# Query, key, value and gates of a hybrid attention block prepared between the input units and kept in DRAM

## What is computed

```python
h = rms_norm(x, g_mix)
q_down, kv_down, k_rope, conv_in, gate_logits = split(h @ w_in)    # 256, 128, 32, 1024, 2048 columns
q  = rms_norm(q_down, g_q_lora) @ w_uq                # 8 heads of 64 + 32 rotary
kv = rms_norm(kv_down, g_kv_lora) @ w_ukv             # 8 heads: 64 of k, 64 of v
k  = concat(k_nope, k_rope of all heads)
q, k = rope(rms_norm(q, g_qk_q)), rope(rms_norm(k, g_qk_k))
y_a = chunk_causal_attention(q, k, v) @ w_o_mla       # blocks of 128 queries, keys up to their own chunk of 64
u   = conv_value * sigmoid(conv_gate)
y_b = silu(layer_norm(depthwise_conv_31(u))) @ w_conv_out
gates = sigmoid(gate_logits + b_gates)                # two of width 1024
x = x + (gates[:D] * y_a + gates[D:] * y_b) @ w_out
x = x + experts(rms_norm(x, g_ffn))                   # 32 experts, two per token
```

## Time and profile before

| | |
|---|---|
| median of 3 runs | 1280.9 us (1279.85 to 1282.06) |
| profiled execution | 1280.47 us, span 1278.4 us |
| TensorE matmul busy | 1178.3 us, 92% of the span |
| VectorE, ScalarE, GpSimd busy | 751.0, 469.2, 198.9 us |
| chain that ended last | TensorE 71%, DMA 12%, ScalarE 4%, VectorE 4% |
| input units, attention, branches | 281, 269, 89 us |

### The profile page before, as it was taken

One profiled execution on the slowest core, in us unless ns is written; L12 is line 12 of the kernel. 1 busy time (PEld: TensorE's weight loads), 2 busy tenths in 40 slices (PEclk: granted clock), 3 DMA queues, 4 the chain that ended last, 5 costly groups with the idle time before them and its releaser, 6 DMA issues.

```text
span 1278.4 us, 14988 instructions
## 1 busy us (share of the span) xinstructions
PE 1178.3 (92%) x5452; PEld 896.4 (70%) x5452; DVE 751.0 (59%) x992; ACT 469.2 (37%) x635; POOL 198.9 (16%) x243
## 2 busy tenths in 40 slices
PE   5999999999968999999899899849999988989996
PEld 5988888887645667767788788746676665666664
DVE  3338999993424455444466434476776656656663
ACT  4432111113443444444232211124555544554552
POOL 4010000000142232220000000011222321222211
PEclk8999999999969999999799999958999999999999
DMA  6011111110100000001330233495999999999980
GB/s 224 1 50 50 49 49 49 49 49 17 42 0 1 1 1 1 1 1 34 131 83 17 90 113 129 169 320 179 324 339 320 304 322 316 334 333 314 308 267 8
DMA packets 101542, 172.28 MB, mean 135 GB/s; under 512 B 11727, under 2 KB 45690, under 8 KB 101498
## 3 DMA queue, kind: packets, MB, share of 16 engines
q1 hardware_dynamic: 91002, 154.86, 35.8%
q0 software_dynamic: 10432, 16.81, 5.4%
q10 hardware_dynamic: 64, 0.02, 0.0%
HBM read 165.35 MB, written 27.26 MB: 151 GB/s over the span
## 4 chain that ended last, share of the span: by engine, by line
PE 71%; DMA 12%; ACT 4%; DVE 4%; issue 4%; POOL 2%; SPq 2%; DVEq 0%; ACTq 0%; POOLq 0%
PE pb L1224 15%; PE pb L1226 15%; PE pb L1225 15%; DMA wgu_raw<-in_w_e_up 11%; PE pb L1506 7%; PE pb L1364 4%; PE pb L1341 4%; PE pb L1353 2%; PE pb L1273 2%; PE pb L1478 2%; PE pb L1283 1%; PE pb L1424 1%; ACT wgu_hi L772 1%; SPq L414 1%; SPq L418 1%
## 5 line engine op out<-in xcount | busy, mean ns | idle before, releaser
L1165 DVE TENSOR_TENSOR wgu_lo<-wgu_raw,wgu_hi 128x2048 fp32r<-128x2048 f32 x72 | 164.7, 2289 | 89.3 <-ACT wgu_hi L772 87.8
L1506 PE MATMUL pb<-wed,midT 128*128 128x512 f32 x288 | 136.5, 618 | 23.1 <-DVE midT L1200 23.0
L873 DVE SCALAR_TENSOR_TENSOR cv<-up,dwc,cv 128x1024 f32<-128x1024 f32 x120 | 154.1, 1284 | 3.7
L1224 PE MATMUL pb<-hT_hi,ws_hi 128*128 128x512 f32 x384 | 151.7, 395 | 0.0
L772 ACT ACTIVATE wgu_hi<-wgu_raw 128x2048 fp32r<-128x2048 f32 x72 | 137.1, 1909 | 38.0 <-DMA wgu_raw<-in_w_e_up 33.8
L1226 PE MATMUL pb<-hT_hi,ws_lo 128*128 128x512 f32 x384 | 149.5, 389 | 0.0
L1225 PE MATMUL pb<-hT_lo,ws_hi 128*128 128x512 f32 x384 | 149.5, 389 | 0.0
L1224 PE MATMUL pb<-wgu_hi,hgT_hi 128*128 128x512 f32 x288 | 130.0, 452 | 0.0
L1506 PEld LDWEIGHTS pb<-wed,midT 128*128 128x128 f32 x288 | 54.6, 196 | 87.2 <-issue 62.5
L1226 PE MATMUL pb<-wgu_hi,hgT_lo 128*128 128x512 f32 x288 | 113.2, 393 | 0.0
L1225 PE MATMUL pb<-wgu_lo,hgT_hi 128*128 128x512 f32 x288 | 112.5, 391 | 0.0
(11 more groups left out here) (281 smaller groups left out, 2019.9 us busy)
## 6 DMA issues: line engine op xcount, KB each, us to landing
wgu_raw<-in_w_e_gate SPq DMA_DIRECT2D x36, 1024.0 KB
wgu_raw<-in_w_e_up SPq DMA_DIRECT2D x36, 1024.0 KB
wed<-in_w_e_down SPq DMA_DIRECT2D x36, 1024.0 KB, 16.3
ws_raw<-in_w_in SPq DMA_DIRECT2D x24, 512.0 KB, 3.9
xs<-in_x SPq DMA_DIRECT2D x8, 512.0 KB, 8.4
wout<-in_w_out SPq DMA_DIRECT2D x1, 4096.0 KB, 12.9
xb<-in_x SPq DMA_DIRECT2D x8, 512.0 KB, 5.2
h_rows<-h SPq DMA_DIRECT2D x8, 512.0 KB, 2.7
```

Source lines behind the costliest of these rows:

```text
L873: i = v.scalar_tensor_tensor(out=cv[:, c, :], in0=src, scalar=w, in1=cv[:, c, :], op0=ALU.mult, op1=ALU.add)
L1165: v.tensor_tensor(wgu_lo[q % SLOTS][:, :, ks, :], wgu_raw[q % SLOTS][:, :, ks, :], wgu_hi[q % 2][:, :, ks, :].bitcast(F32), ALU.subtract). ...
L1224: t_.matmul(out, w(0), m(0), start=start, stop=False)
L1506: m = t_.matmul(pb[:, 4 + h, :], midT[:, f, :], wed[q][:, f, h * 512:(h + 1) * 512], start=(f == 0), stop=(f == 1))
```

## The change

- Preparation (now `prep`) of tile t starts in unit 1+2t and runs over 32 steps, in the order of `PREP` at the steps `PREP_STEP`. TensorE has two banks for it (6 and 7, in turn), VectorE's program has its pieces two steps later (`PREP_LAG`) among the taps, ScalarE's has them after the split for the unit after next. The squares are now made in PSUM, and VectorE sums them in halves.
- q, k and v go to staging tiles (`qst`, `kst`, `vst`), are stored to DRAM, and are loaded again for attention (q two tiles at a time). Gates go through two staging rows (`gst`) to DRAM and come back for the branches.
- The scores of heads 0 and 1 go into unit 23 at its steps 2 and 6, behind the convolution's layer norm; the exponentials of both follow the convolution's swish on ScalarE.
- Attention has no preparation left. `attn_T` transposes the output tile; ScalarE and VectorE split it straight from PSUM into `aT`. The convolution's result is split at heads 9 to 12. The first branch unit starts with its convolution half; the last output tile is transposed between its two halves.
- The rotary angles and tables are computed ahead of unit 0's evacuation and right after it, rather than at units 1 and 19.
- The unit loops are written out; the matmuls of the units are the same.

```diff
+        PREP = ("qdT", "q0", "q1", "kv0", "kv1", "qT0", "qT1", "kT0", "kT1")
+        PREP_STEP = (0, 3, 6, 9, 12, 22, 24, 28, 30)
+        PREP_UNIT, PREP_LAG = 1, 2
+        prep_at = {STEPS * PREP_UNIT + 2 * STEPS * t + g: (k, t) for t in range(NTILE) for k, g in zip(PREP, PREP_STEP)}
...
 # SyncE
+                store_gate(u - 4)
+                sp.wait_ge(u_hi, u - 1)
+                sp.wait_ge(u_lo, u - 1)
+                load_unit(u % 2, unit_col(u))
+                store_prep(u - 4)
...
+            sp.wait_ge(ln_y, NC)
+            sp.dma_start(vv[:, :, :], v_d.rearrange("t p c -> p t c")).then_inc(v_in, 16)
...
+            sp.wait_ge(pv_ok, NTILE * HEADS)
...
+            load_gates(0)
+            load_gates(1)
 # ScalarE
                 if u + 2 < IN_UNITS:
                     unit_hi(u + 2)
+                for s in range(STEPS):
+                    if STEPS * (u + 1) + s in prep_at:
+                        prep(*prep_at[STEPS * (u + 1) + s])
 # VectorE
                 if u + 2 < IN_UNITS:
                     unit_lo(u + 2)
+                if u == 0:
+                    rotary_tables()
...
+                fresh = max(0, target - taps_done)
+                for s in range(STEPS):
+                    for k in range(taps_done + fresh * s // STEPS, taps_done + fresh * (s + 1) // STEPS):
+                        tap(k)
+                    if STEPS * (u + 1) + s - PREP_LAG in prep_at:
+                        prep(*prep_at[STEPS * (u + 1) + s - PREP_LAG])
 # TensorE
+                    if kind == "q0":
+                        bb, cc = prep_slot("qdT", t)
+                        pe.wait_ge(prep_free[bb], cc)
...
+            def unit(u):
+                b = u % 2
                 for f in range(2):
                     for k in range(KD):
+                        if STEPS * u + f * KD + k in prep_at:
+                            prep(*prep_at[STEPS * u + f * KD + k])
+                        if u == IN_UNITS - 1 and f == 0 and k in (2, 6):
+                            pe.wait_ge(ln_sd, 1)
+                            pe.wait_ge(ln_y, 1)
+                            scores(k // 4)
                         i = three(pb[:, 2 * b + 2 + f, :], lambda s: ws[s][:, b, k, :], lambda s: hT[s][:, k, f * 512:(f + 1) * 512], k == 0, k == KD - 1)
...
                 probs_T(n)
-                for k, t in slots(j, h, 0):
-                    misc(k, t)
                 if n + 2 < NTILE * HEADS:
                     scores(n + 2)
-                for k, t in slots(j, h, 1):
-                    misc(k, t)
+                if j and h == 2:
+                    attn_T(j - 1)
                 pv(n)
...
+            branch(0, 1)
+            attn_T(NTILE - 1)
+            pe.wait_ge(at_lo, NTILE)
+            branch(0, 0).then_inc(u_mm, 1)
```

More of the change, by code:

```diff
@@ L60 @@
 TAPS_PER_UNIT = 7
+STEPS = 2 * KD
 LO_SPLIT = 5
@@ L324, in build, with prep_slot @@
         EARLY = ((NTILE - 1) * HEADS + 4, (NTILE - 1) * HEADS + 5)
[L326 to L337, removed]
+        CONV_SPLIT = (9, 10, 11, 12)
+        PREP = ("qdT", "q0", "q1", "kv0", "kv1", "qT0", "qT1", "kT0", "kT1")
+        PREP_STEP = (0, 3, 6, 9, 12, 22, 24, 28, 30)
+        PREP_UNIT, PREP_LAG = 1, 2
+        prep_at = {STEPS * PREP_UNIT + 2 * STEPS * t + g: (k, t) for t in range(NTILE) for k, g in zip(PREP, PREP_STEP)}
+        def prep_slot(kind, t):
+            n = len(PREP) * t + PREP.index(kind)
+            return n % 2, n // 2 + 1
+        SBANK = (0, 6)
         SMALL_VECS = ((V_GM, g_mix, 8), (V_BG, b_gates, 16), (V_BD, b_dw, 4), (V_GL, g_conv_ln, 4),
@@ L384, in _, with unit_col, prep_freed, store_prep @@
-            sp.wait_ge(u_hi, IN_UNITS)
-            sp.wait_ge(u_lo, IN_UNITS)
+            def unit_col(u):
+                if u < GLU_UNITS:
+                    return (VALUE_COL if u % 2 else GATE_COL) + (u // 2) * P
+                return LOGIT_COL + (u - GLU_UNITS) * P
+            def prep_freed(*pieces):
+                for piece in pieces:
+                    b, count = prep_slot(*piece)
+                    sp.wait_ge(prep_free[b], count)
+            def store_prep(u):
+                t, late = divmod(u - PREP_UNIT, 2)
+                if not 0 <= t < NTILE:
+                    return
+                if late:
+                    prep_freed(("qT0", t), ("qT1", t))
+                    sp.dma_start(qT_d[t], qst[0:QK, :]).then_inc(q_out, 16)
+                    prep_freed(("kT0", t), ("kT1", t))
+                    sp.dma_start(kT_d[t], kst[0:QK, :]).then_inc(k_out, 16)
+                else:
+                    prep_freed(("kv0", t), ("kv1", t))
+                    sp.dma_start(v_d[t], vst[:, :]).then_inc(v_out, 16)
@@ L1283, in misc, with scores @@
                         i = t_.transpose(M[0:QK, h * P:(h + 1) * P], src[:, h0 + h, :], ident[:, :])
[L1284 to L1290 removed]
+                i.then_inc(prep_ps[b], 1)
+            def scores(n):
+                j, h = divmod(n, HEADS)
+                w = (j + 1) * P
+                if h == 0:
+                    pe.wait_ge(q_in[j % 2], 16 * (j // 2 + 1))
+                    pe.wait_ge(k_in[j], 16)
+                if n >= 2:
+                    pe.wait_ge(ex_ok, n - 1)
+                S = banks(SBANK[n % 2], 2)
+                for f in range(0, w, 512):
+                    e = min(w, f + 512)
+                    t_.matmul(S[:, f:e], qT[0:QK, j % 2, h * P:(h + 1) * P], kT[0:QK, f // P:e // P, h * P:(h + 1) * P], start=True, stop=(e < w))
+                t_.matmul(S[:, w - P:w], mrow[0:1, 0, :], mrow[0:1, 1, :], start=False, stop=True).then_inc(sc_ok, 1)
@@ L1308, in _ @@
-            for u in range(LN_UNIT, IN_UNITS):
-                pe.wait_ge(u_lo, u + 1)
-                pe.wait_ge(u_ev, u - 1)
-                if u < IN_UNITS - 1:
-                    unit(u % 2)
-                else:
-                    pe.wait_ge(ln_sd, 1)
-                    unit(u % 2, {(0, 0): "qdT", (0, 4): "q0", (0, 7): "q1", (1, 2): "kv0", (1, 5): "kv1"})
+            for u in range(IN_UNITS):
+                pe.wait_ge(u_lo, u + 1)
+                if u >= 2:
+                    pe.wait_ge(u_ev, u - 1)
+                unit(u)
```

441 lines of the change are left out of this document (219 added, 222 removed).

## The result

The changed kernel takes 1323 us (median of 4 runs, 1320.4 to 1340.9) against 1281.5 for the kernel before (4 runs, 1279.9 to 1285.9): the ratio is 1.030, with a 95% interval of 1.027 to 1.034. The forecast was 1318, in 1284 to 1340. The total came out; two of its terms did not, and their errors cancelled, which is luck.

A forecast was written before the change was run, and what follows sets the result against it. TensorE was taken to bound the input units and late attention, while early attention waits at a slow clock. 1280.5 + 94.1 (units) - 81.3 (attention) + 24.5 (GpSimd contention) = 1317.8, or 1318 us against the median; range 1284 to 1340.

The forecast's parts named there:

- The wait for `qdT`: Input units: TensorE idles before the first q matmul, 3.8 us for each of tiles 1 to 7, 7.8 for tile 0.
- Falls of the clock in the units: Input units: each wait brings TensorE's clock down, about 1.5 us of loss each, 12 us in all.
- Work moved: Input units: preparation moved onto TensorE adds 46.9 us; with early scores, waits and clock losses the units grow 94.1 us.
- the case without contention: Input units: GpSimd does not hold up VectorE, so a tile's pair of units takes 33.7 us.
- GpSimd beside the taps: Input units: GpSimd's work holds up VectorE's taps, 3.5 us a tile between bounds 0 and 5, 24.5 us in all.
- Attention without preparation: Attention stage: lasts 187.7 us instead of 269.0, a saving of 81.3 us.
- early attention at the slow clock: Attention tiles 0 and 1: 4.7 + 9.4 us of TensorE work double; part of a rival reaching 1342, chance 0.08.
- its own test: Attention stage: the prediction would be wrong if attention's length fell outside 180 to 200 us.
- waits alone: Input units: rival with the waits but VectorE not held up by GpSimd, total 1294 us, chance 0.25.

## Why the prediction was right, and where it was not

**The wait for `qdT`: right.** 7.8 us for tile 0, as forecast; 3.0 to 3.5 instead of 3.8 for the others, 30.7 instead of 34.4 in all. The order on VectorE and the limit by the split are in the trace as read from the earlier trace rows. Removing it gave 28 us in the units.

**Falls of the clock in the units: right.** 0.96 of 377 us are 2 x 0.04 x 377 = 30 us at 1.2 GHz, worth 15; without the waits 0.99 of 348, worth 3.5. The forecast had 12.

**Work moved: right.** A pair of units is 33.7 us, the figure that the prediction worked out for the case without contention. The units grew from 281.3 (70.4 to 351.7) to 376.2 us (71.9 to 448.1), by 94.9 against 94.1.

**GpSimd beside the taps, 24.5 us: wrong, it is nothing.** The step that failed is the count of VectorE's time in a pair of units. It took 8.7 us of GpSimd's work a tile as lost to VectorE; the traces show 13.1 us for all eight tiles, and none of it in the pair of units. GpSimd bore more: its products, sums and powers take 107 us in the changed units where the same ones took 70 in attention before. Its product of 512 elements takes 1782 ns where it took 1043, while the one of 768 is at 1471 in both:

```profile
L575 POOL TENSOR_TENSOR kn<-kn,ssh 128x512 f32<-128x512 f32 x8 | 14.3, 1782 | 0.6
...
L565 POOL TENSOR_TENSOR qn<-qn,ssh 128x768 f32<-128x768 f32 x8 | 11.8, 1471 | 0.6
```

The Trainium skill (SBUF — State Buffer, section SBUF: two separate sides) has the pair of ports held for a whole instruction by whoever starts first. The trace agrees that VectorE can be kept waiting (its longest tap is 2432 ns with GpSimd's operations, 1639 without them), and shows that a rule on who waits is no price. The prediction chose 3.5 between 0 and 5 us a tile by the nearest row; the row told of a single meeting, and not of how much slack VectorE has.

**Attention without preparation, 187.7 us: wrong by about as much the other way.** It took 228.8 us in the profile. The step that failed is the sum by 0.585 us a block, which is the full clock's, for tiles 1 to 4. The text had seen the low clock of early attention and laid it to the preparation and its gaps; it stood only in a rival ("early attention at the slow clock"), priced by tiles 0 and 1. That preparation, whose matmuls stood in these heads, had helped to hold the clock up fits the runs with added work, but was not tested by itself. With the clock held at 1.00 the sum is right to 3 us (190.3 with the last output tile). In the unprofiled runs the term is smaller: they are 19 us shorter than the profiled one, so by an estimate that puts all of this difference into attention its excess there is 228.8 - 187.7 - 19 = 22 us.

**The total** was right by luck: a term of 24.5 us that isn't there stood for about 28 that are (by the same estimate 22 in attention, 2 up to the end of the units, 4 behind attention): 1294 + 28 = 1322. By its own test ("wrong if attention is outside 180 to 200 us") the prediction's account was wrong. The rival *waits alone*, at 1294, had the units right and the total wrong by 29.

## What to carry to other kernels

Before work is moved out of a stage, look at the granted clock of that stage and ask what in it keeps the clock up: short dependent steps with little between them may go with a low clock, and the stage then isn't "TensorE-bound at full speed" however busy it looks. When work is moved in between other work, put what it waits for first in the follower's order; here one step less of lag and three more before q, made together, were worth 28 us in the units. And check a sum stage by stage, not by its total.

## What the runs showed that was not expected

The clock fell after gaps of under 1 us each (0.76 and 0.39; 0.37 to 0.92; 0.33 and 0.23), in short heads. The Trainium skill (TensorE: Matmul & The Clock Gate, section A second HAM failure mode: psum-queue depth-cycling) tells of another kernel in which small idle times between groups of matmuls make the clock swing; the falls agree with it. Such gaps are not the whole of it: with the same 0.33 and 0.23 us in the same instructions the clock fell in one run and held in another, and in the kernel before it was at 1.00 while TensorE was busy for 6.40 of 8 us. The stay does not agree with it either: here the clock lay at 1.2 GHz for 88 to 112 us while the trace shows almost no idle time, and came back 3.8 or 11.6 us after each head had been given 0.7 us (at full clock) more to do. What makes the difference isn't settled. Neither the width of the matmuls nor their type is the answer, as far as the runs with narrow and with float32 work go (the narrow one tests only the fall, the float32 one only the return). By the mean clocks the time at 1.2 GHz differs from execution to execution, and so does the whole: 1307 and 1350 us for one kernel.
